# Two-block transformer on one core: bias rows read as long runs, wide units in the last two feed-forward stages, and the input split straight out of PSUM

## The reference, cut to what matters

```python
def swiglu(x, w_gate, w_up, w_down):
    return (jax.nn.silu(x @ w_gate) * (x @ w_up)) @ w_down

# neighbourhood attention, per row of the grid
bias = rpb[:, dr[None, :, None] + NA_KH - 1, dc[:, None, :] + NA_KW - 1]
s = s + bias.astype(jnp.float32)[None]

def _conv_ffn(h, w_up, ffn_conv, ffn_conv_bias, w_down):
    gate, up = _split(h @ w_up, (D_FF_2, D_FF_2))
    gate = _dwconv(gate, ffn_conv) + ffn_conv_bias
    return (jax.nn.silu(gate) * up) @ w_down
```

## Time and profile before

| | us |
|---|---|
| median of 3 runs | 2278.19 (2277.61 to 2287.46) |
| profiled execution, device time | 2279.91 |
| its span, first to last instruction | 2278.1 |
| TensorE busy | 2196.8 |
| DVE busy | 1617.0 |
| ACT busy | 1138.6 |
| POOL busy | 188.6 |

### The profile page before, as it was taken

One profiled execution on the slowest core, in us unless ns is written; L12 is line 12 of the kernel. 1 busy time (PEld: TensorE's weight loads), 2 busy tenths in 40 slices (PEclk: granted clock), 3 DMA queues, 4 the chain that ended last, 5 costly groups with the idle time before them and its releaser, 6 DMA issues.

```text
span 2278.1 us, 37348 instructions
## 1 busy us (share of the span) xinstructions
PE 2196.8 (96%) x14476; PEld 1983.1 (87%) x14476; DVE 1617.0 (71%) x2477; ACT 1138.6 (50%) x1735; POOL 188.6 (8%) x156
## 2 busy tenths in 40 slices
PE   8999999999999999999999999999999999999998
PEld 7888969888788888797888989898998989898997
DVE  5668656766686675577667779867777779867766
ACT  4445465544454445555444475435434475335443
POOL 0000000012200000000000107310000006310000
PEclk9999999999999999999999999999999999999999
DMA  7554424399955554344554442214555442214554
GB/s 259 186 186 165 166 74 166 137 198 202 202 204 187 186 181 167 113 165 155 194 187 166 153 148 93 93 38 161 187 188 185 149 148 100 86 38 176 185 184 147
DMA packets 52680, 359.06 MB, mean 158 GB/s; under 512 B 6416, under 2 KB 6800, under 8 KB 11088
## 3 DMA queue, kind: packets, MB, share of 16 engines
q1 hardware_dynamic: 47216, 341.86, 41.6%
q0 software_dynamic: 4064, 12.32, 4.5%
q10 hardware_dynamic: 1280, 3.19, 0.4%
HBM read 356.29 MB, written 1.05 MB: 157 GB/s over the span
## 4 chain that ended last, share of the span: by engine, by line
PE 79%; DVE 10%; ACT 4%; DMA 4%; issue 2%; SPq 0%; DVEq 0%; ACTq 0%
PE tile L777 22%; PE acc L822 19%; PE tile L789 13%; PE tile L790 7%; PE tile L802 7%; PE tile L1142 4%; DMA ring<-weights 4%; DVE ring_lo L1907 3%; PE tile L1339 2%; ACT w_hi L1410 2%; PE tile L984 1%; PE tile L954 1%; DVE work L2459 1%; DVE work L2430 1%; DVE work L2428 0%
## 5 line engine op out<-in xcount | busy, mean ns | idle before, releaser
L1907 DVE TENSOR_TENSOR ring_lo<-ring,w_hi 128x1024 fp32r<-128x1024 f32 x648 | 791.0, 1241 | 510.5 <-ACT w_hi L1410 507.6
L1410 ACT ACTIVATE w_hi<-ring 128x1024 fp32r<-128x1024 f32 x648 | 657.9, 1054 | 799.9 <-DMA ring<-weights 583.6
L777 PE MATMUL tile<-xT_parts,w_hi 128*128 128x256 f32 x3200 | 584.6, 285 | 11.3 <-DVE xT_parts L2339 6.0
L777 PEld LDWEIGHTS tile<-xT_parts,w_hi 128*128 128x128 f32 x3200 | 501.8, 192 | 17.3 <-issue 8.9
L789 PE MATMUL tile<-xT_parts,w_hi 128*128 128x512 f32 x1408 | 500.6, 399 | 4.3 <-DVE xT_parts L1898 2.0
L777 PE MATMUL tile<-xT_parts,ring_lo 128*128 128x256 f32 x1600 | 453.5, 283 | 0.0
L790 PE MATMUL tile<-xT_parts,ring_lo 128*128 128x256 f32 x1408 | 396.0, 281 | 0.0
L789 PEld LDWEIGHTS tile<-xT_parts,w_hi 128*128 128x128 f32 x1408 | 265.3, 188 | 71.9 <-issue 5.2
L777 PEld LDWEIGHTS tile<-xT_parts,ring_lo 128*128 128x128 f32 x1600 | 307.8, 192 | 0.0
L790 PEld LDWEIGHTS tile<-xT_parts,ring_lo 128*128 128x128 f32 x1408 | 266.7, 189 | 1.3
L822 PE MATMUL acc<-w_hi,hidden_hi 128*128 128x512 f32 x528 | 207.5, 393 | 5.7 <-DVE ring_lo L1907 3.0
(11 more groups left out here) (278 smaller groups left out, 2835.8 us busy)
## 6 DMA issues: line engine op xcount, KB each, us to landing
ring<-weights SPq DMA_DIRECT2D x324, 1024.0 KB, 4.8
work<-ln_g_rows POOLq DMA_DIRECT2D x8, 512.0 KB, 5.2
work<-ln_b_rows POOLq DMA_DIRECT2D x8, 512.0 KB, 6.2
work<-rpb POOLq DMA_DIRECT2D x32, 96.0 KB, 7.7
x<-x_in SPq DMA_DIRECT2D x1, 1024.0 KB, 7.9
work<-mem_in ACTq DMA_DIRECT2D x1, 1024.0 KB, 6.8
out<-x SPq DMA_DIRECT2D x2, 512.0 KB, 2.6
work<-hmask_in ACTq DMA_DIRECT2D x1, 840.0 KB, 8.5
```

The lines of the kernel that those rows point to most:

```text
L777: j = mm(ps[:, f * S:(f + 1) * S], w[a][:, k, :], x2[b][:, k, :], start=(k == 0 and i == 0), stop=(k == KT - 1 and i == 2))
L1410: A(high_of(u, h), half_of(ring, u, h), ACT.Copy).then_inc(sems["w_hi"], 1)
L1907: V.tensor_tensor(half_of(ring_lo, u, h), half_of(ring, u, h), high_of(u, h).bitcast(F32), ALU.subtract).then_inc(sems["w_lo"], 1)
```

## The change

1. The bias is fetched in two transfers for all 16 heads, 64 x 16 x 219 numbers each (runs of 876 bytes), into `bias_runs`; POOL's 16 additions then read overlapping windows of it and write `grid_bias`.
2. `two_tiles` is true for `ffn(4)` and `ffn(5)` too. The convolution reads the summed gate in `hidden` (SBUF), and `product` reads the summed up in `up_low`.
3. At the start ACT and DVE split x from the PSUM banks, without the copy to `xT`, and the first unit's halves are split between the pairs of x. The constants are loaded in two transfers, the first 256 columns on ACT's queue, the others on SP's behind the three units.
4. Filler: at the start 4 before x instead of 9 behind its transposes; in `rms_transposes` 21 for 16; in `turned` none.

```diff
 def two_tiles(n):
-    return n < 4
+    return n < 6
@@ SP
+            sp.dma_start(const[:, S:], consts[:, S:]).then_inc(sems["tables_in"], 16)
@@ PE
-                keep_busy(first[:, 0:S], 16 if r == 0 else 4)
+                keep_busy(first[:, 0:S], 21 if r == 0 else 4)
...
-                    if a == 0 and j == 0:
-                        keep_busy(ps[:, 0:S], 1)
...
+            keep_busy(acc[0][:, 0:S], 4)
             pe.wait_ge(sems["x_in"], 16)
             transposes(plan.tile["x"], x)
-            keep_busy(acc[0][:, 0:S], 9)
 
             ffn(0, "x")
+            pe.wait_ge(sems["tables_in"], 16)
@@ ACT
-            act.dma_start(const[:, :], consts).then_inc(sems["const_in"], 16)
+            act.dma_start(const[:, 0:S], consts[:, 0:S]).then_inc(sems["const_in"], 16)
...
                 def gate(f, more):
+                    t = t0 + 2 * f
+                    act.wait_ge(sems["half_used"], more * 6 + plan.ready[t][1])
+                    A(hidden[:, f % 4, :], bank[t % NB][:, 0:S], ACT.Copy).then_inc(sems["small_out"], 1)
                     if conv_first:
 
                         act.wait_ge(sems["conv_done"], more * 4 + FT * (n - 4) + f + 1)
...
             for q in range(4):
-                take(plan.tile["x"] + q, pair(xT, q))
-            for h in range(2):
-                split_half(0, h)
-            split_norm("x", plan.tile["x"])
+                act.wait_ge(*ready(plan.tile["x"] + q))
+                split_pair("x", q, bank[(plan.tile["x"] + q) % NB][:, :])
+                if q % 2 == 1:
+                    split_half(0, q // 2)
@@ DVE
+                    if f is not None:
+                        gate_sum(f, more)
                     if f is not None and conv_first:
                         convolve(n, f, more)
-                    if f is not None and two_tiles(n):
-                        gate_sum(f, more)
...
             def convolve(n, f, more):
...
-                dve.wait_ge(sems["unit_used"], more * 6 + plan.ready[t0 + f][1])
+                t = t0 + 2 * f
+                dve.wait_ge(tile_taken[t % NB], more * 2 + t // NB + 1)
@@ POOL
+                    pool.wait_ge(sems["unit_used"], plan.unit[("ffn", 1)] + 2)
+                    for half in range(2):
+                        src = bass.AP(rpb.tensor, rpb.offset + (1 - half + 4) * 31 - 48,
+                                      [[1, GRID], [465, NHEADS], [1, BIAS_RUN]])
+                        pool.dma_start(bias_runs[half * GRID:(half + 1) * GRID, :, 0:BIAS_RUN], src).then_inc(sems["rpb_in"], 16)
+                    pool.wait_ge(sems["rpb_in"], 16 * 2)
                     for h in range(NHEADS):
-                        pool.wait_ge(sems["unit_used"], plan.unit[("ffn", 1)] + 2 + 3 * h // 2)
...
+                        pool.wait_ge(sems["unit_used"], plan.unit[("ffn", 1)] + 6 + 3 * h // 2)
+                        first = bias_runs[:, h, 0:1]
+                        windows = bass.AP(first.tensor, first.offset, [first.ap[0], [31, 6], [1, GRID]])
+                        i = G.tensor_tensor(grid_bias[:, h], windows, gb, ALU.add)
```

More of the change, by code:

```diff
@@ L51 @@
 GRID = 64
+BIAS_RUN = 5 * 31 + 64
 NA_KH, NA_KW = 8, 16
@@ L578, in build @@
         grid_bias = region(23552, NHEADS, 6, GRID)
+        bias_runs = region(12288, NHEADS, BIAS_RUN + 1)
         acc = [ctx.enter_context(nc.psum_tensor(f"acc{b}", [P, 512], F32)) for b in range(4)]
@@ L1426, in gate @@
                     else:
-                        t = t0 + 2 * f
-                        act.wait_ge(sems["half_used"], more * 6 + plan.ready[t][1])
-                        A(hidden[:, f % 4, :], bank[t % NB][:, 0:S], ACT.Copy).then_inc(sems["small_out"], 1)
                         act.wait_ge(tile_taken[t % NB], more * 2 + t // NB + 1)
@@ L2225, in lower_bounds @@
                 step.link(V.tensor_scalar(omlb[:, :, :], lb[:, :, :], -r, r, ALU.mult, ALU.add))
-            for h in range(2):
-                split_half(0, h)
-            split_operand("x", xT)
+            for q in range(4):
+                t = plan.tile["x"] + q
+                split_pair("x", q, bank[t % NB][:, :])
+                dve.wait_ge(sems["x_lo"], 4 * plan.sets["x"] + q + 1)
+                dve.sem_inc(tile_taken[t % NB], 1)
+                if q % 2 == 1:
+                    split_half(0, q // 2)
             for h in range(2):
@@ L2780, in _ @@
                     gb = table("grid").unsqueeze(1).to_broadcast([P, 6, GRID])
[L2782 to L2795 removed]
+                    pool.wait_ge(sems["unit_used"], plan.unit[("ffn", 1)] + 2)
[4 more added lines that the diff above has]
+                    pool.wait_ge(sems["rpb_in"], 16 * 2)
+                    for h in range(NHEADS):
+                        pool.wait_ge(sems["unit_used"], plan.unit[("ffn", 1)] + 6 + 3 * h // 2)
+                        first = bias_runs[:, h, 0:1]
+                        windows = bass.AP(first.tensor, first.offset, [first.ap[0], [31, 6], [1, GRID]])
+                        i = G.tensor_tensor(grid_bias[:, h], windows, gb, ALU.add)
+                        if h < NHEADS - 1:
+                            step.did(i)
                     i.then_inc(sems["bias_ready"], 1)
```

29 lines of the change are left out of this document (6 added, 23 removed).

## The result

| | us |
|---|---|
| before, median of 6 runs | 2280.51 (2277.61 to 2287.46) |
| after, median of 6 runs | 2267.90 (2265.14 to 2269.79) |
| after / before | 0.9943, 95% interval 0.9929 to 0.9958 |
| span of the profiled execution after | 2265.6 |

The change gains 12.6 us by the medians (2280.51 - 2267.90) and 12.5 us by the two profiled executions (2278.1 - 2265.6). The forecast sum was 12.2 us. The parts of the sum are another matter.

A forecast was written before the change was run, and what follows sets the result against it. TensorE was taken as the bound, busy 2196.8 of 2278.1 us. Terms 6.0 + 2.2 + 1.6 + 1.9 + 0.5 = 12.2 us off 2278.2 gave 2266.0 us, range 2259 to 2274 us.

The forecast's parts named there:

- Bias runs: In ffn(1): fewer, longer bias runs remove TensorE's 7.5 us of waits for 1.5 us; gain 6.0 us, bounds -1 and +7.5.
- the sharing of the engines: In ffn(1): a unit sharing DMA engines with the bias runs costs 0 to 2.5 us; 1.5 us taken.
- my 9 to 12: In ffn(1): a unit that shares the engines with the bias runs lands after 9 to 12 us.
- the 9.5 us that I allowed: In ffn(1): a unit's load may take some 9.5 us before TensorE notices.
- The rival that a unit is shut out: In ffn(1): the bias block makes one unit 8 us late, so no gain there; 2272 us, chance 0.2.
- My price of 0.10 us a run: Bias transfers before: 73 us per DMA engine over 720 runs, so 0.10 us a run.
- my 13 us: Bias block in ffn(1): 128 runs per engine take 13 us if a run costs the same as before.
- Wide units: ffn(4) and ffn(5): laps save 4.2 us, last D units lose 2.0 us; net gain 2.2 us, bounds 0 and 4.2.
- Start: Up to unit 0: begins 3.5 us sooner, half clock loses 1.9 us; net gain 1.6 us, bounds 0 and 4.
- my 1.7 us: At the start: without 0.69 MB of constants beside x, x and unit 0 land 1.7 us sooner.
- Norm r = 0: Second network's first norm: five more fillers keep the clock up; gain 1.9 us, bounds 0 and 1.9.
- Filler before the transposed probabilities: First attention: removing eight fillers, 4 us, gains only 0.5 us as waits grow; bounds -3 and +1.

The follow-up runs named there:

- the pieces: Changed kernel with bias runs in eight pairs of transfers behind every third ffn(1) unit, instead of one pair: 2259.91 us, in another group 2262.19 us.

## Why the prediction was right, and where only its sum was

- **Bias runs (6.0 forecast, 3.3 measured).** The step that failed is the sharing of the engines. I took the wait from the median unit of the earlier trace rows, 2.7 us late, and charged 1.5 us. But a median over a whole feed-forward tells nothing of a block: the unit issued in the middle of it landed only when the block was through, after 12.1 us, just past the top of my 9 to 12. And a load may take less than the 9.5 us that I allowed (my own terms give 11.2 - 2 = 9.2): from this unit's landing at 466.0 us to TensorE's start at 468.44 us pass 2.4 us for the splits, and TensorE had been ready 3.6 us before that start, so a load of about 8.5 us (12.1 - 3.6) is the most that goes unnoticed. The second price of a long wait, up to 2.6 us of slow clock, I had charged at the norm and at the start, but not here. The rival that a unit is shut out was half right: the unit was 7.3 us later than the 4.8 us of an undisturbed one and the place cost 6.4 us, but `ffn(1)` still gained. My price of 0.10 us a run was too high: the packets of the block took 0.067 us a run, 8.6 us an engine and not 13. That its transfers landed after 13.0 us in the median agrees with my 13 us by luck, since weights moved in the same time. The row of before also undervalued what could be had: 9.2 us, not 7.5. The Trainium skill says that an engine changes between queues only at whole packets ("DMA: Bandwidth & Descriptors", section "Queues, rings and completion order"), and I expected longer packets. In bytes they grew, from 2.0 KB on average (2.95 MB in 1440 packets) to 4.0 KB, but each took less time, 0.82 us before and 0.31 us after. So longer packets don't explain the late unit, and why the block held it up and 16 short transfers didn't, no run here shows.
- **Wide units (2.2, measured 2.4 to 3.2).** Laps of 16.79 us and 0.9 us in front of each last D unit, as worked out. The four G units ahead of the first lap gained up to 0.2 us each, and I had counted 0.1.
- **Start (1.6, measured 4.8).** Three steps failed. The constants took more from the transfers than my 1.7 us: x landed 2.6 us sooner than before (6.1 for 8.7 us) and unit 0 3.4 us sooner (9.3 for 12.7 us, where I had 11). So unit 0's landing wasn't what the start waited for: ACT splits it at 10.06 us, behind the second pair of x, and TensorE starts at 12.42 instead of 13.6. And the idle time was 1.6 us, where I had 4 us and a loss of 1.9, because the transposes, late behind the filler, ran to 10.8 us; the clock stayed up. With a gap of 2.1 to 2.4 us, in eight further executions, it fell in one; with 3.16 us it fell.
- **Norm r = 0 (1.9, measured 1.7 to 2.2).** Right in mechanism and size, though I misread the end of the slow stretch: 0.67 in the microsecond from 1259 us puts it at 1259.7, not 1259.3.
- **Filler before the transposed probabilities (0.5, measured 0.5).** Right, but only among executions with the same clock. I had said that no second fall would come in that attention, and none did; but in the kernel after the one fall there lasted 6.8 us in place of 3.4.
- What I had named as wrong (a unit landing after 15 us or more, a wait in every lap, unit 0 not before 16 us) didn't come. Of what I had said the profile would show, four things didn't either: waits of TensorE in `ffn(1)` under 2 us (3.6), no unit landing later than 12 us (12.1), unit 0 begun at 13 to 14 us (12.42), and the start's slow clock.

That the total came out was in good part luck: the start gave 3.2 us more than forecast and the wide form 1.0 us, the bias 2.7 us less, and a fall of the clock by chance took 1.2 us in layer 1's attention.

## What to carry to other kernels

Count what a transfer block does to the next load of the stream, not to the median one: if a load may take some 8.5 us and the block needs about 13 us to pass, cut it, here into 16 transfers that made TensorE wait nowhere. Filler pays only inside a measured gap, and only where no other engine is late next; three fillers cost 1.3 us without a gap, four in front of a later wait gained nothing, and filler ahead of x held up the transposes. Compare two traces by a ledger of start times, or 3.2 us too much in one stage and 2.7 us too little in another pass for a right number.

## What the runs showed of the hardware

**Falls of the clock come and go with the same program.** In 14 profiled executions (before, after, and twelve of the experiments) each fall of the granted clock ahead of the last D unit lasted about 3.4 or 6.8 us. Behind a wait of 1.83 us, at the same instruction of layer 1's attention, the clock fell in 5 of the 13 executions after the change and not in the one before; it cost 1.2 to 1.4 us a time. In front of `ffn(3)`, behind 2.05 us, it fell in 4 of the 12 without filler there, and in the first mixer, at about 1400 us behind 1.84 us, in 4 of 14. In the first attention, behind four waits of 0.8 to 1.8 us within 17 us, it fell in 10 of the 11 executions after the change that have no filler in that gap, in three of them for 6.8 us. At the norm r = 0 it fell both times behind 3.0 and 3.2 us, and never behind 1.05 us. So in these traces idle time over 3 us nearly always had its price (of the six such gaps only one, 3.57 us long, had none), and 1.8 us of it was a gamble. The Trainium skill ("TensorE: Matmul & The Clock Gate", section "Part 1: The HAM clock gate") says that the lower clock is the default and that activity releases it; that every fall looked at here stands behind idle time agrees. Why one execution falls and another doesn't isn't settled here. In one case it accounts for the difference between two runs of one kernel: the two executions of the pieces differ by 2.8 us in span, and the falls at 922 and 1400 us, of which the first execution had neither, cost 1.3 and 1.5 us by the ledger. Whether it explains the spread of 3 to 10 us in general isn't shown.
